# Mixture-of-experts blocks of 32 rows on four column tiles of TensorE, with experts in a sorted order

## The reference

```
grp_sel = argmax(h @ w_grp + b_grp)                    # one of 4 groups
top_p, top_i = top_k(softmax(logits of that group), 2) # two of its 8 experts
y = sum over the two: gate * (silu(x @ w_gate[e]) * (x @ w_up[e])) @ w_down[e]
```

```
layer 0: 334 231 205 174 146 145 128 109 102 84 82 73 71 56 52 51 49 49 45 44 44 43 39 39 36 30 25 22 18 15 12 7
layer 1: 548 178 177 176 156 91 87 70 66 65 57 55 42 41 37 25 25 23 21 16 14 12 12 10 10 9 6 6 5 4 2 2
```

## Time and profile before

| | us |
|---|---|
| profiled execution, own time | 5788.05 |
| its span, first to last instruction | 5785.7 |
| median of the three timed executions | 5775.29 |
| experts phase, layer 0 (2776.1 to 3543.6) | 767.5 |
| experts phase, layer 1 (4958.6 to 5705.0) | 746.4 |

### The profile page before, as it was taken

How to read it: one execution, slowest core, us unless ns; L and a number is a source line. 1 busy time by engine, 2 the same in 40 slices (tenths; PEclk the granted TensorE clock), 3 DMA queues, 4 the chain that set the end, 5 groups by cost and what they waited for, 6 DMA issues and landing times. The chain is left out here.

```text
span 5785.7 us, 71070 instructions
## 1 busy us (share of the span) xinstructions
PE 4182.2 (72%) x23474; PEld 2739.1 (47%) x23475; DVE 2196.7 (38%) x4254; ACT 1422.0 (25%) x3188; POOL 639.3 (11%) x1135
## 2 busy tenths in 40 slices
PE   5597599395876949574499983598199955497893
PEld 1385377284765838453133321487056644132331
DVE  0312544666556656624000002411677733200003
ACT  0210254343333424212011110210056622011111
POOL 0000000131322313300100002000300010100001
PEclk9798799697988969786799996799599977799997
DMA  9421100101010010133886697322510023799943
GB/s 336 147 86 68 62 9 9 38 1 25 10 25 10 0 34 1 46 128 109 312 339 235 228 377 282 118 89 76 193 49 10 11 98 105 274 364 397 374 165 145
DMA packets 350063, 778.83 MB, mean 135 GB/s; under 512 B 52000, under 2 KB 95284, under 8 KB 349796
## 3 DMA queue, kind: packets, MB, share of 16 engines
q1 hardware_dynamic: 297640, 624.64, 30.1%
q10 hardware_dynamic: 37696, 103.04, 4.6%
q0 software_dynamic: 14544, 48.79, 2.4%
HBM read 656.45 MB, written 122.58 MB: 135 GB/s over the span
## 5 line engine op out<-in xcount | busy, mean ns | idle before, releaser
L2306 PE MATMUL ex_bG<-ex_w,ex_xT 128*64 x880 | 424.7, 639 | 134.5 <-SPq L2227 77.3
L2306 PE MATMUL ex_bY<-ex_w,ex_aT 128*64 x880 | 392.6, 599 | 74.5 <-DVE ex_aT L2369 59.7
L2309 PE MATMUL ex_bG<-ex_w,ex_xT 128*64 128x512 f32 x880 | 424.7, 639 | 0.0
L367 PE MATMUL p_acc<-hT,p_wh 128*128 128x512 f32 (+1 forms) x1056 | 376.2, 356 | 24.6 <-DVE p_wl L379 24.6
L2309 PE MATMUL ex_bY<-ex_w,ex_aT 128*64 128x512 f32 x880 | 392.8, 600 | 0.0
L2306 PE MATMUL ex_bU<-ex_w,ex_xT 128*64 x880 | 386.6, 592 | 0.0
L2309 PE MATMUL ex_bU<-ex_w,ex_xT 128*64 128x512 f32 x880 | 386.6, 592 | 0.0
L2367 DVE TENSOR_TENSOR ex_a<-ex_sg,ex_bU 128x512 f32<-128x512 f32 x55 | 37.9, 688 | 917.9 <-PE ex_bU L2309 917.9
L367 PE MATMUL p_acc<-hT_rest,p_wh 128*128 128x512 f32 (+1 forms) x1056 | 375.7, 356 | 0.0
L367 PE MATMUL p_acc<-hT,p_wl 128*128 128x512 f32 (+1 forms) x1056 | 375.2, 355 | 0.0
L2306 PEld LDWEIGHTS ex_bG<-ex_w,ex_xT 128*64 128x64 f32 x880 | 127.9, 148 | 415.3 <-issue 415.3
(11 more groups left out here) (362 smaller groups left out, 8841.4 us busy)
## 6 DMA issues: line engine op xcount, KB each, us to landing
ex_w<-in_moe_w_gate SPq DMA_DIRECT2D x64, 2048.0 KB, 17.8
ex_w<-in_moe_w_up SPq DMA_DIRECT2D x64, 2048.0 KB, 21.2
ex_w<-in_moe_w_down SPq DMA_DIRECT2D x64, 2048.0 KB, 18.1
mods_w<-in_mod_w SPq DMA_DIRECT2D x24, 2048.0 KB, 13.0
projT_dram<-p_o ACTq DMA_DIRECT2D x44, 640.0 KB, 2.9
yb_dram<-ex_y ACTq DMA_DIRECT2D x55, 512.0 KB, 6.3
p_w<-in_od_w_in SPq DMA_DIRECT2D x12, 1024.0 KB, 5.1
n_x<-x_dram SPq DMA_DIRECT2D x20, 512.0 KB, 4.1
```

What stands on the lines that cost most here:

```text
L367: mm = nc.tensor.matmul(acc[u % 2][c][:, 0:n], a[:, u // 2, k, at], b[:, k, t0:t0 + n], start=k == 0 and x == 0, stop=k == KT - 1 and x == 2)
L2306: nc.tensor.matmul(bank[0:BR, :], stationary[:, k, 0:BR], w[:, ds(slot0 + (offset + k * n), 512)], start=k == 0, stop=k == tiles - 1)
L2309: m = nc.tensor.matmul(bank[BR:P, :], stationary[:, k, BR:P], w[:, at:at + 512], start=k == 0, stop=k == tiles - 1)
```

## The change

- Blocks have 32 rows. A block is worked on alone: its gate and up products are four column tiles of 32 columns each (two halves of gate, two of up), with 256 weight columns moving through each; its down product is four tiles of 256 output columns.
- Rows are gathered as 128 pieces of 1 KB (32 rows, four quarters), the result is stored the same way; h is written to memory with its columns in another order so that the pieces fit. Weights lie in the tile with eight (gate, up) or two (down) neighbouring rows of the matrix on one partition, so that a run in memory is 16 KB or 8 KB instead of 2 KB or 4 KB.
- Turning rows is no longer a transpose but a product with the identity (`turn_rows`, `turn_hidden`) on the same four column tiles.
- The loop is a software pipeline of two blocks: hidden products of block b, down product of b-1, turned rows of b+2, turned hidden rows of b. ACT does silu and the stores alone, VectorE all copies. The result has four buffers, the other tiles two.
- Routing sorts the experts by their number of rows on the chip: largest, smallest, second largest, second smallest, and so on. Experts are loaded and worked on in that order, and all 32 are loaded, as before. The number of blocks is rounded to 4n+1: 97 in layer 0 and 85 in layer 1.

The diff, cut to its core (of the new streams only the loop bodies and the functions that they call stand here):

```diff
--- before.py
+++ after.py
+XG, XC = 4, D // 4
...
-                        nc.vector.tensor_tensor(h[:, u, :], h0[:, u, :], mod[:, cond, 0, :], ALU.add).then_inc(h_done, 1)
+                        nc.vector.tensor_tensor(placed(h[:, u, :]), natural(h0[:, u, :]), natural(mod[:, cond, 0, :]), ALU.add).then_inc(h_done, 1)
...
-BR = 64
-NPM = (2 * TOK + NE * (BR - 1)) // BR // 2 + 1
-NPT = NPM + 1
-NBT = 2 * NPT
+BR = 32
+CAP = TOK // BR
+NBM = (2 * TOK + NE * (BR - 1)) // BR
+NBT = NBM + 4
+MQ = (NBM + 2) // 4
 WR = 3
-CAP = TOK // BR
-
-
-T_NP, T_EXP, T_PEND, T_CODE = 0, 1, 1 + NE, 1 + 2 * NE
-T_COLS = T_CODE + NPT
+
+
+T_QUAD, T_EXP, T_PEND, T_CODE = 0, 1, 1 + NE, 1 + 2 * NE
+T_COLS = T_CODE + NBT
...
-                c.did(V.tensor_scalar(steps[:, 0:2 * NPT], iota[:, 0:2 * NPT], float(BR), None, ALU.mult))
+                c.did(V.tensor_scalar(steps[:, 0:CAP], iota[:, 0:CAP], float(BR), None, ALU.mult))
                 tally(col(NB), rows_(count, NE, CAP), cols_(steps[:, 0:CAP], NE, CAP), ALU.is_gt, NE, CAP)
-                c.did(V.tensor_tensor_scan(col(BEND), ones[:, 0:NE], col(NB), 0.0, ALU.mult, ALU.add))
-                c.did(V.tensor_tensor(col(BST), col(BEND), col(NB), ALU.subtract))
+                c.did(V.scalar_tensor_tensor(out=col(KEY), in0=count, scalar=-float(NE), in1=iota[:, 0:NE], op0=ALU.mult, op1=ALU.add))
+                tally(col(POS), cols_(col(KEY), NE, NE), rows_(col(KEY), NE, NE), ALU.is_lt, NE, NE)
+                c.did(V.tensor_scalar(col(POS), col(POS), 2.0, None, ALU.mult))
+                c.did(V.tensor_scalar(col(ORD), col(POS), -1.0, 2.0 * NE - 1.0, ALU.mult, ALU.add))
+                c.did(V.tensor_tensor(col(ORD), col(ORD), col(POS), ALU.min))
+                tally(col(BST), cols_(col(ORD), NE, NE), rows_(col(ORD), NE, NE), ALU.is_lt, NE, NE, cols_(col(NB), NE, NE))
...
+                dve.wait_ge(back_in, 16)
+                nc.vector.tensor_scalar(back4[:, :, :], back[:, :].rearrange("n (o t) -> n o t", o=1).to_broadcast([NBT, XG, BR]), float(XG), None, ALU.mult).then_inc(spread_done, 1)
...
-                    sp.dma_start(w[:, u * WCOLS + at:u * WCOLS + at + kk * n].rearrange("p (o k n) -> p o k n", o=1, n=n),
-                                 wv(name)[:, ds(e, 1), :, :]).then_inc(w_in[part][u], 16)
+                    to = w[:, u * WCOLS + at:u * WCOLS + at + kk * n]
+                    if part < 2:
+                        sp.dma_start(to.rearrange("p (o k n) -> p o k n", o=1, n=n),
+                                     d[name][layer].rearrange("e (p k) n -> p e k n", k=kk)[:, ds(e, 1), :, :]).then_inc(w_in[part][u], 16)
+                    else:
+                        sp.dma_start(to.rearrange("p (o g n) -> p o g n", o=1, g=2),
+                                     d[name][layer].rearrange("e (g p h) n -> p e g (h n)", g=2, h=2)[:, ds(e, 1), :, :]).then_inc(w_in[part][u], 16)
...
+                def gather(b, p):
+                    nc.gpsimd.tensor_copy(idx[:, p:p + 1], tok[:, ds(b, 1)]).then_inc(idx_done, 1)
+                    pool.wait_ge(idx_done, b + 1)
+                    pool.sem_inc(go, 1)
+                    nc.gpsimd.indirect_dma_start(x[:, p, :], None, pieces, bass.IndirectOffsetOnAxis(idx[:, p:p + 1], 0)).then_inc(x_in[p], 16)
+                gather(0, 0)
+                gather(1, 1)
+                pool.wait_ge(xtr, 1)
+                gather(2, 0)
                 with pool.Fori(0, n) as i:
+                    for u in PAR:
+                        pool.wait_ge(xtr, 2 * i + u + 2)
+                        gather(2 * i + u + 3, 1 - u)
...
+                def turn_rows(p, landed, b=None):
+                    pe.wait_ge(x_in[p], 16 * landed)
+                    if b is not None:
+                        pe.wait_ge(a_done, b + 1)
+                    for e in range(2):
+                        for g in range(4):
+                            at = e * P + g * BR
+                            t = nc.tensor.matmul(bX[p][g * BR:(g + 1) * BR, e * P:(e + 1) * P], x[:, p, at:at + BR], ident[:, :], start=True, stop=True)
+                    t.then_inc(xtr, 1)
+                def place(b):
+                    code = load(pe, ds(b + T_CODE, 1), WR * (NE + 1) - 1, WR)
+                    return code // WR, code % WR
+                def hidden(p, u):
+                    for c in range(XG):
+                        for e in range(2):
+                            for g in range(4):
+                                at = u * WCOLS + (0, UP)[g // 2] + (2 * c + e) * EH + g % 2 * HC
+                                m = nc.tensor.matmul(bH[p][g * BR:(g + 1) * BR, 0:HC], xT[:, p, e, c, :], w[:, at:at + HC],
+                                                     start=c == 0 and e == 0, stop=c == XG - 1 and e == 1)
+                    m.then_inc(h_done, 1)
+                def down(p, u):
+                    for k in range(HT):
+                        for g in range(4):
+                            at = u * WCOLS + DOWN + k * D + g * XC
+                            m = nc.tensor.matmul(bY[p][g * BR:(g + 1) * BR, 0:XC], aT[:, p, k % 2, k // 2, :], w[:, at:at + XC], start=k == 0, stop=k == HT - 1)
+                    m.then_inc(y_done, 1)
+                def turn_hidden(p):
+                    for h in range(2):
+                        for g in range(4):
+                            t = nc.tensor.matmul(bA[p][g * BR:(g + 1) * BR, h * 2 * BR:(h + 1) * 2 * BR], a[:, p, h, g * BR:(g + 1) * BR], ident[:, 2 * BR:P], start=True, stop=True)
+                    t.then_inc(atr, 1)
+                def block_down(b, p):
+                    need, slot = place(b)
+                    pe.wait_ge(w_ready[2], need)
+                    pe.wait_ge(aT_done, b + 1)
+                    for u in range(WR):
+                        with pe.If(slot == u):
+                            down(p, u)
+                turn_rows(0, 1)
+                turn_rows(1, 1)
+                pe.wait_ge(w_ready[0], 1)
+                pe.wait_ge(w_ready[1], 1)
+                pe.wait_ge(xT_done, 1)
+                hidden(0, 0)
+                turn_rows(0, 2, 0)
+                turn_hidden(0)
                 with pe.Fori(0, n) as i:
+                    for q in PAR:
+                        b, p = 2 * i + q + 1, 1 - q
+                        need, slot = place(b)
+                        for part in range(2):
+                            pe.wait_ge(w_ready[part], need)
+                        pe.wait_ge(xT_done, b + 1)
                         for u in range(WR):
+                            with pe.If(slot == u):
+                                hidden(p, u)
+                        block_down(b - 1, 1 - p)
+                        turn_rows(p, i + q + 2, b)
+                        turn_hidden(p)
+                block_down(2 * n, 0)
...
-                act.sem_inc(ended, 1)
+                    for u in range(4):
+                        gated(4 * i + u + 1, (u + 1) % 2)
+                        store(4 * i + u, u)
...
+                def rows_turned(b, p):
+                    dve.wait_ge(xtr, b + 1)
+                    nc.vector.tensor_copy(xT[:, p, :, :, :].rearrange("p e c t -> p (e c t)"), bX[p][:, 0:2 * P]).then_inc(xT_done, 1)
+                def product(b, p):
+                    dve.wait_ge(sg_done, b + 1)
+                    nc.vector.tensor_tensor(a[2 * BR:P, p, :, :], sg[2 * BR:P, p, :].rearrange("p (m h) -> p h m", h=2),
+                                            bH[p][2 * BR:P, 0:HC].rearrange("p (m h) -> p h m", h=2), ALU.mult).then_inc(a_done, 1)
+                def hidden_turned(b, p):
+                    dve.wait_ge(atr, b + 1)
+                    nc.vector.tensor_copy(aT[:, p, :, :, :].rearrange("p h g t -> p (h g t)"), bA[p][:, 0:4 * BR]).then_inc(aT_done, 1)
+                def result(b, u, i):
+                    dve.wait_ge(y_done, b + 1)
+                    dve.wait_ge(y_out[u], 16 * i + 16)
+                    nc.vector.tensor_copy(y[:, u, :], bY[u % 2][:, 0:XC]).then_inc(ye_done, 1)
+                rows_turned(0, 0)
+                rows_turned(1, 1)
+                product(0, 0)
+                hidden_turned(0, 0)
+                rows_turned(2, 0)
                 with dve.Fori(0, n) as i:
+                    for u in range(4):
+                        b, p = 4 * i + u + 1, (u + 1) % 2
+                        product(b, p)
+                        hidden_turned(b, p)
+                        rows_turned(b + 2, p)
+                        result(b - 1, u, i)```

TensorE, head of the experts loop, before: from the loop's start to the first gate products of a round.

```order
3573 L2295 UNCONDITIONAL_BRANCH
3574 L2295 ISA
3575 L2208 TENSOR_LOAD table
3576 L2208 ISA x2
3577 L2312 REGISTER_ALU
3578 L2313 ISA
3579 L2304 REGISTER_ALU
3580 L2304 COMPARE_AND_BRANCH
3581 L2306 ISA
3582 L2306 MATMUL ex_bG<-ex_w,ex_xT 64x512
3583 L2309 MATMUL ex_bG<-ex_w,ex_xT 64x512
```

(3 more changed lines are left out.)

203 lines of the change are left out of this document (76 added, 127 removed).

## The result

The changed kernel takes 5862.41 us (median, 5858.70 to 5868.73) against 5780.74 us of the kernel before on the same chip: ratio 1.0142, 95% interval 1.0125 to 1.0160. Slower, as the forecast's 5804 said, and in its range of 5640 to 5930, but the loss is about three times the one forecast. The profiled execution took 5863.66 us (span 5861.8); the forecast for it was 5817.

A forecast was written before the change was run, and what follows sets the result against it. No one engine bounds the experts phases throughout: TensorE and DMA alternate. Experts +5, routing +17 and norm +7 make +29 us on the profiled 5788, so 5817; the median, 13 below, 5804; range 5640 to 5930.

The forecast's parts named there:

- Start and end: Experts phases: first product 18 us into the phase, end 5 us as now, one last block of 8 in layer 1.
- Products: Experts blocks: four tiles side by side, 0.215 us a set, 5.16 a block; 195 us less work from less padding.
- The forecast's rival: Experts products: four tiles don't run side by side; at 0.28 us a set, kernel about 5980; chance 13%.
- Control: Experts loop: sequencer outlasts a queue of 36 instructions, stalling TensorE 0.57 and 1.33 us, 1.9 us a block.
- queue of 64: TensorE's queue in the experts loop: by the skill's depth of 64, a block about 6.8 us, kernel about 5660.
- Outside: Routing and norm ahead of the experts phases: 17 us more for routing and 7 for norm, 24 in all.
- the half I took: Norm's strided writes: 0 to 14 us more over 18 instructions; half, 7 us, taken.
- The routing's share: Routing ahead of the experts: 8.6 us longer a layer, 17 us for two.
- Layer 0: Its experts phase: 18 + 757 + 5 = 780 us, with 97 blocks of 7.8 us and TensorE seldom waiting for weights.
- Layer 1: Its experts phase: 18 + 351 + 357 + 13 = 739 us: 45 blocks, 21 experts' weights at 17 us, end.
- Gathers ... Cost nothing; if a copy were late: Experts loop: gathers land in 4.0 to 9.0 us, have 15; late copy or landing rival: 5946 us, chance 7%.
- signs of being right: Experts phases: sets 0.21 to 0.22 us, blocks 7.8, layer 1 weight waits 50 to 60, layer 0 clock 1.00.

The follow-up runs named there:

- e1_cut4: The changed kernel with each weight transfer issued in four pieces, so that weight packets are 4 KB: 5879.67 us.
- e13_cut2: The changed kernel with weight transfers in pieces of 8 KB throughout and nothing else changed: 5864.30 us.

## Why the prediction was off

The direction (slower had a chance of 50%, faster of 38%), the mechanism of control and the time outside the phases were right. What failed is the step *Start and end* with the two sums built on it, 18 + 757 + 5 and 18 + 351 + 357 + 13: they cost the first blocks like any other and the end as before. Point by point:

- *Products.* Forecast 0.215 us a set, measured 0.217. The forecast's rival took a gain of 3.07 times from the Trainium skill's page "TensorE: Matmul & The Clock Gate" (section "Measured speedup vs the span model"). The page measures it on four row tiles of 512 columns, not on column tiles; carried over to these it gave an estimate of 0.28, and these rows disagree with that.
- *Control.* Forecast stalls of 0.57 and 1.33 us and a block of 7.7 to 7.8. Measured idle times are 0.20 us in the median ahead of `ex_bY` (0 to 0.8 for most blocks) and 1.1 ahead of `ex_bH` (0.7 to 1.6), 1.5 us a block in layer 0 where the forecast had 1.9; the usual block takes 7.6 to 7.8. The two doses, one table read less and one branch more, confirm the mechanism. At the table load ahead of the down products at most 40 of the hidden products' instructions are still to start, near the 36 of the earlier trace rows. By the queue of 64 that the Trainium skill gives (same page, section on the array as 16 sub-arrays) the block would have taken an estimated 6.8 us; the usual one is far from that, and the shortest in the trace takes 6.9. (In the sum, the second load's 1.18 us is 0.05 more than its parts, 0.66 + 0.32 + 0.15.)
- *Outside.* Forecast 24 us, measured 24.4. In layer 0 the last transposes of norm start at 2691.56 instead of 2686.88, 4.7 us later; 1.3 of this was there at norm's first transposes already (2654.19 instead of 2652.88). VectorE's strided write, in layer 0:

```profile
L291 DVE TENSOR_TENSOR nb_h<-nb_h,nb_mod x10: 1904/1926/1932, 2652.2 to 2689.5; 128x1024 f32<-128x1024 f32 x10
```

  That is 0.70 us more than the earlier trace rows, near the upper bound (0.23 us for 320 elements make 0.74 for 1024, not the 0.77 of the forecast) rather than the half I took. Ten of them are 7.0 us, of which at most 3.4 show. The routing's share is then 14.1 less 4.7, 9.4 (forecast 8.6).
- *Layer 0*, forecast 780, measured 789.6: the first product is 3.2 earlier (14.8), two of the first three blocks are 13.7 longer (code; some 9 of it is idle time beyond the usual, the rest products at the half clock after the gaps), the other 94 together 2.8 shorter, and the last block with the end 2.3 longer.
- *Layer 1*, forecast 739, measured 776.0. The first product 2.5 earlier, the first three blocks 16.4 longer (code), blocks 4 to 45 8.4 shorter (7.60 us each). Then 370.5 us to the last expert's first product where 21 x 17 is 357: 13.5 more, 17.6 an expert. Of this stretch the profile gives TensorE's waits to stuck stores, not to weights; `e1_cut4` and `e13_cut2` show that late weights lay just behind them, but how the 13.5 divide stays open. Behind it 31.0 us instead of 13: the two padding blocks that I had counted in the 85 come *after* the last weights, where nothing hides them, and I had put one block there.

The sum of these is +0 outside, +30 for the first pass through the code, +18 and +2 at the ends, +13.5 for weights and stores, -11 for blocks faster than 7.8 and -6 for the first products: about 47 us, the miss of the profiled execution (5863.66 against 5817). The last 11 to 12 us of the median's miss are mine as well. I carried over that a profile lies 13 us above the median, and here it lies at it.

So the terms that failed are two I had costed at nothing or too little: the start, with code for three slots and two parities fetched in the first pass (costed at 7.8 us a block like the rest, 30 us short), and the end of layer 1 (13 us, measured 31.0). The step "Gathers ... Cost nothing; if a copy were late" missed a third: a store is also an instruction on ACT, and silu stands behind it. In this kernel its cost was mostly covered by late weights. Runs with another order, where it was not covered, showed it.

Of the forecast's signs of being right, two failed as well: the 50 to 60 us of waits for weights in the second half of layer 1 are 1.1 us in the profile, with 67.3 us for `ex_a` in their place, and the clock in layer 0 is 0.97 over the phase, 1.00 only between its first and last 100 us. The gap ahead of `ex_bH` also carries the copy's name where I had expected "issue". And that 5862 lies in the range of 5640 to 5930 is partly luck: the upper part of the range stood for blocks of up to 8.6 us, and the blocks took 7.75; the time got there by the start and the end.

## What to carry over

When products are cut shorter, count the sequencer's instructions against what its queue holds in time. Move table reads to where the queue is full, and don't trust the releaser that a profile names for a gap that repeats in each block without a run that tests it. A small store on an engine that also computes is a risk when weights in large packets fill the DMA engines: look at the issue's own longest time, and test weight packet size and order together, as each hides what the other does. Padding and first passes cost most where nothing overlaps them.

## What the hardware showed that I had not expected

- Stores of 1 KB packets beside weight packets of 8 and 16 KB at full rate landed up to 57 us after their issue (60 with one table read), and their issue held ACT for up to 12.5 us; beside packets of 4 KB no issue took more than 1.5 us, and no store landed later than 11.7 us. The larger packets move 391 to 403 GB/s, those of 4 KB 359 to 380, in the same stretches.
- In the first pass through code single branches took 1.9 to 5.1 us (0.20 after it) as 16 KB instruction packets came in, six at the start of each layer's experts phase; smaller weight packets did not change it (2.4 to 4.9 us), 16 KB more code made the start 3.5 to 5 us longer. The granted clock fell to 0.5 for 6.8 us at each of two such gaps in a layer.
- One store of 128 packets occupies ACT for 0.555 us even when idle; the one of before took 0.343.
- 265 of 266 store issues over 1.5 us began with three earlier stores, 384 packets, not yet landed, and none with fewer than two. Which limit of the queue that is, and why a third of the 400 issues that began so did not stick, was not told apart.
